# The first output unit of a hybrid attention layer computed in fp32 from unscaled inputs, and one more row tile turned by DMA

## The reference, cut to what matters

```python
h = x * rsqrt(mean(x*x) + 1e-6) * norm_pre_g          # x: 512 rows x 1024, fp32
u = h @ w_in                                          # 1024 x 4096, eight groups of 512 columns
dq, dk, dv, dg, mq, mk, mv, mg = split(u)
a = rmsnorm(softmax-difference attention(dq, dk, dv) + bias) * silu(dg)
b = block attention(mq, mk, mv) + bias, * silu(mg)
out = x + rmsnorm(concat(a, b) @ w_out) * norm_post_g
```

## Time and profile before

| | |
|---|---|
| median of 3 executions | 257.85 us (257.16 to 259.13) |
| the profiled execution | 258.5 us, span of its trace 256.7 us |
| TensorE (PE) busy | 246.4 us, 96% |
| VectorE (DVE) busy | 174.9 us, 68% |
| ScalarE (ACT) busy | 144.4 us, 56% |
| GpSimd (POOL) busy | 32.9 us, 13% |

### The profile page before, as it was taken

One profiled execution on the slowest core, in us unless ns is written; L12 is line 12 of the kernel. 1 busy time (PEld: TensorE's weight loads), 2 busy tenths in 40 slices (PEclk: granted clock), 3 DMA queues, 4 the chain that ended last, 5 costly groups with the idle time before them and its releaser, 6 DMA issues.

```text
span 256.7 us, 4437 instructions
## 1 busy us (share of the span) xinstructions
PE 246.4 (96%) x1589; PEld 123.5 (48%) x1589; DVE 174.9 (68%) x382; ACT 144.4 (56%) x337; POOL 32.9 (13%) x77
## 2 busy tenths in 40 slices
PE   6899999999999999999989999999999999999990
PEld 6544444445444545544455444444444444554570
DVE  1787766367559688868787777867888784936313
ACT  3986557156365667574676686485677553721110
POOL 2139300000000230041041041000000000110101
PEclk9999999999999999999999999999999999999997
DMA  6979997897045434534535763586569954596222
GB/s 221 402 250 243 277 277 282 250 360 213 21 51 138 146 112 132 122 106 112 107 110 132 121 189 103 125 221 149 146 162 184 248 148 79 99 164 206 47 84 83
DMA packets 59626, 42.47 MB, mean 165 GB/s; under 512 B 45760, under 2 KB 46024, under 8 KB 59604
## 3 DMA queue, kind: packets, MB, share of 16 engines
q1 hardware_dynamic: 59604, 42.19, 62.0%
HBM read 29.04 MB, written 2.13 MB: 121 GB/s over the span
## 4 chain that ended last, share of the span: by engine, by line
PE 70%; DVE 8%; ACT 8%; DMA 8%; issue 3%; SPq 1%; POOL 1%; DVEq 0%; POOLq 0%; ACTq 0%
PE unit_ps L562 57%; PE score_ps L597 5%; PE o_ps L618 4%; DMA pt<-arena 4%; DMA stage<-in_w_in_dram 3%; ACT arena L747 2%; PE unit_ps L578 2%; ACT w_hi L707 2%; DVE w_lo L840 2%; ACT junk L693 1%; DVE w_lo L838 1%; ACT w_hi L706 1%; DVE arena L917 1%; SPq L378 1%; PE score_ps L670 1%
## 5 line engine op out<-in xcount | busy, mean ns | idle before, releaser
L562 PE MATMUL unit_ps<-area,w_hi 128*128 128x512 f16 x256 | 76.2, 380 | 0.0
L562 PE MATMUL unit_ps<-w_hi,area 128*128 128x512 f16 x224 | 70.5, 380 | 0.9 <-DVE w_lo L840 0.8
L747 ACT ACTIVATE arena<-arena,negmax 128x512 f32<-128x512 f32 (+3 forms) x64 | 35.4, 554 | 44.2 <-DVE negmax L917 44.0
L562 PE MATMUL unit_ps<-area,w_lo 128*128 128x512 f16 x128 | 48.5, 379 | 0.0
L562 PE MATMUL unit_ps<-w_lo,area 128*128 128x512 f16 x112 | 42.5, 379 | 0.0
L562 PEld LDWEIGHTS unit_ps<-area,w_hi 128*128 128x128 f16 x256 | 24.0, 98 | 27.3 <-issue 1.1
L562 PEld LDWEIGHTS unit_ps<-w_hi,area 128*128 128x128 f16 x224 | 21.8, 98 | 27.3 <-issue 2.0
L917 DVE CUSTOM_DVE_ANT_0 arena<-score_ps,strips 128x512 f32<-128x512 f32 (+3 forms) x64 | 28.6, 485 | 8.5 <-PE score_ps L597 8.3
L838 DVE SCALAR_TENSOR_TENSOR w_lo<-stage,g_cols,w_hi 128x512 f16<-128x512 f32 x32 | 24.2, 756 | 14.0 <-ACT w_hi L707 13.8
L706 ACT ACTIVATE w_hi<-stage,g_cols 128x512 f16<-128x512 f32 x32 | 22.7, 711 | 7.7 <-DMA stage<-in_w_in_dram 7.6
L840 DVE SCALAR_TENSOR_TENSOR w_lo<-stage,g_cols,w_hi 128x512 f16<-128x512 f32 x32 | 24.9, 777 | 0.0
(11 more groups left out here) (98 smaller groups left out, 334.2 us busy)
## 6 DMA issues: line engine op xcount, KB each, us to landing
stage<-in_w_in_dram SPq DMA_DIRECT2D x32, 512.0 KB, 4.2
stage<-in_w_out_dram SPq DMA_DIRECT2D x8, 512.0 KB, 3.8
arena<-in_x_dram SPq DMA_DIRECT2D x4, 512.0 KB, 7.7
strips<-bias_rows SPq DMA_DIRECT2D x1, 2048.0 KB, 11.8
stage<-in_x_dram SPq DMA_DIRECT2D x4, 512.0 KB, 3.5
out_dram<-area SPq DMA_DIRECT2D x3, 512.0 KB, 3.3
strips<-bias_rows SPq DMA_DIRECT2D x1, 1024.0 KB, 8.8
g_row<-in_norm_post_g_dram SPq DMA_DIRECT2D x1, 512.0 KB, 12.4
```

What stands on the lines that cost most here:

```text
L562: last = nc.tensor.matmul(bank, a, b, start=(k == 0 and n == 0), stop=(k == KT - 1 and n == 2))
L747: nc.scalar.activation(probs[:, i % 2, m, 0:n], probs[:, i % 2, m, 0:n], ACT.Exp, bias=negmax[:, i, m:m + 1], scale=-1.0, accum_out=sums[: ...
```

## The change

- Unit 0 is 8 fp32 products (`first_quarter`): x tile 0 is transposed by TensorE as loaded (no row factor), VectorE multiplies it by `g_cols` on the way out of PSUM into `x_first` (`x_weigh`), and the moving operand is the weights as loaded, in the stage buffers. The row factor (times 1/64, `first_scale`) is applied when the unit is evicted. Loads 4 to 7 also wait until the unit has read the stage.
- `ht` of tile 0 is no longer made on this way: tile 0 is scaled, split and turned by DMA like tiles 2 and 3, after them; it is first read by unit 4.
- Unit 1 takes its high products first, quarter by quarter, like units 2 and 3 (`late_lower_unit`).
- All four row tiles have their squares shared between ScalarE and VectorE.
- The warm-up products are 5 and 2 in place of 8, 2 and 8; tile 0's transposes wait for x alone.
- norm_pre_g is loaded from ScalarE's queue. The loads of lambda and of the subln weights stand behind the transposes of tile 0, and VectorE's dot products of lambda follow unit 3. Splits in the prologue come a unit later.

Its core:

```diff
-    WARM_UP = (8, 2, 8)
+    WARM_UP = (5, 2)
...
-    SPLIT_AT_UNIT = [[4], [5, 6], [7], [8, 9], [10], [11, 12], [13]]
+    SPLIT_AT_UNIT = [[], [4], [5, 6], [7], [8, 9], [10, 11], [12, 13]]
...
-    X_PARTS = [2] + [1] * (TILES - 1)
...
+    X_TURNED = [2, 3, 0]
...
+        x_first = gates[:, 1, 0:2, :].rearrange("p t (k s) -> p (t k) s", s=P)
+        def x_columns(t):
+            return score_ps[:, 2 * t:2 * t + 2, :].rearrange("p b (k s) -> p (b k) s", s=P)
+        def x_half_rows(t):
+            return x_halves[:, t % 2, :, :]
...
             def load_quarter(n):
                 if n >= 4:
                     sp.wait_ge(split_lo, n - 3)
+                if 4 <= n < 7:
+                    sp.wait_ge(first_read, n - 3)
+                elif n == 7:
+                    sp.wait_ge(unit_done, 1)
...
             def turn_x(t, h):
...
+                sp.wait_ge(xn_lo_ready if h else xn_hi_ready, X_TURNED.index(t) + 1)
+                sp.dma_start_transpose(ht[:, h, :, t * P:(t + 1) * P], x_half_rows(t)[:, h, :])\
+                    .then_inc(x_turned[t][h], 16)
...
@@ -392,16 +398,18 @@
...
             with nc.allow_non_contiguous_dma(reason="32 x 12 table, transposed once"):
                 sp.dma_start(rel_t, rel_bias.rearrange("b h -> h b")).then_inc(rel_loaded, 16)
-            sp.dma_start(lam_in[:, :, :], diff_lambda[0].partition_broadcast(P)).then_inc(small_loaded, 16)
-            sp.dma_start(subln[:, :], diff_subln_g[0].partition_broadcast(P)).then_inc(small_loaded, 16)
...
             for h in range(2):
                 turn_x(2, h)
             load_quarter(6)
+            for h in range(2):
+                turn_x(3, h)
             load_quarter(7)
             for h in range(2):
-                turn_x(3, h)
+                turn_x(0, h)
+            sp.dma_start(lam_in[:, :, :], diff_lambda[0].partition_broadcast(P)).then_inc(small_loaded, 16)
+            sp.dma_start(subln[:, :], diff_subln_g[0].partition_broadcast(P)).then_inc(small_loaded, 16)
             load_quarter(8)
             sp.wait_ge(row_built, 1)
             sp.dma_start(bias_rows.ap(), row_sb).then_inc(rows_stored, 16)
...
...
-                                            ALU.add, ALU.mult).then_inc(x_mean, 1)
+                pool.wait_ge(x_half_squared, t + 1)
+                nc.gpsimd.tensor_tensor(x_ms[:, t:t + 1], x_sq[:, t:t + 1], x_half_sq[:, t:t + 1], ALU.add)\
+                    .then_inc(x_mean, 1)
                 pool.wait_ge(x_mean, t + 1)
                 nc.gpsimd.tensor_tensor(x_rstd[:, t:t + 1], x_ms[:, t:t + 1], minus_half[:, 0:1],
                                         ALU.pow).then_inc(x_rstd_ready, 1)
+                if t == 0:
+                    pool.wait_ge(x_rstd_ready, 1)
+                    nc.gpsimd.tensor_scalar(first_scale[:, :], x_rstd[:, 0:1], U_SCALE, 1.0, ALU.mult,
+                                            ALU.mult).then_inc(first_scale_ready, 1)
...
+            def x_transposes(t, ks, done):
+                for k in ks:
+                    last = nc.tensor.transpose(score_ps[:, 2 * t + k // 4, (k % 4) * P:(k % 4 + 1) * P],
                                                x_sb[:, t, k * P:(k + 1) * P], ident[:, :])
-                last.then_inc(xt_ready, 1)
+                last.then_inc(done, 1)
...
+                        for t in (range(TILES) if kind in "qk" else [i]):
+                            if t == 1:
+                                pe.wait_ge(ht_ready, 1)
+                            else:
+                                pe.wait_ge(x_turned[t][0], 16)
+                                pe.wait_ge(x_turned[t][1], 16)
...
-                if (u, q) == (0, 2):
-                    pe.wait_ge(ht_ready, 2)
                 pe.wait_ge(split_lo, 4 * g + q + 1)
...
-            def turned_unit(u):
+            def first_quarter(q):
+                pe.wait_ge(x_first_ready, q // 2 + 1)
+                pe.wait_ge(w_loaded[q], 16)
+                for k in (2 * q, 2 * q + 1):
+                    cols = slice(k % 2 * WIDTH, (k % 2 + 1) * WIDTH)
+                    last = nc.tensor.matmul(unit_ps[:, 0, :], x_first[:, k, :], stage[:, q, cols], start=(k == 0),
+                                            stop=(k == KT - 1))
+                last.then_inc(first_read if q < 3 else unit_done, 1)
+            def late_lower_unit(u):
                 _, half, i, g = unit_of(u)
                 bank = unit_ps[:, u % 2, :]
                 rows = slice(i * P, (i + 1) * P)
-                pe.wait_ge(unit_freed, u - 1)
-                pe.wait_ge(split_lo, 4 * (g + 1))
-                for h, b in ((0, w_hi), (0, w_lo), (1, w_hi)):
-                    if b is w_hi:
-                        pe.wait_ge(x_turned[i - 2][h], 16)
-                    for k in range(KT):
-                        last = nc.tensor.matmul(bank, ht[:, h, k, rows], b[:, g % 3, k, :],
-                                                start=(k == 0 and h == 0 and b is w_hi), stop=(k == KT - 1 and h == 1))
+                if u >= 2:
+                    pe.wait_ge(unit_freed, u - 1)
+                if i == 1:
+                    pe.wait_ge(ht_hi_ready, 1)
+                else:
+                    pe.wait_ge(x_turned[i][0], 16)
+                for q in range(4):
+                    pe.wait_ge(split_lo, 4 * g + q + 1)
+                    for k in (2 * q, 2 * q + 1):
+                        for b in (w_hi, w_lo):
+                            nc.tensor.matmul(bank, ht[:, 0, k, rows], b[:, g % 3, k, :],
+                                             start=(k == 0 and b is w_hi), stop=False)
+                if i == 1:
+                    pe.wait_ge(ht_ready, 1)
+                else:
+                    pe.wait_ge(x_turned[i][1], 16)
+                for k in range(KT):
+                    last = nc.tensor.matmul(bank, ht[:, 1, k, rows], w_hi[:, g % 3, k, :], start=False,
+                                            stop=(k == KT - 1))
                 last.then_inc(unit_done, 1)
...
             warm_up(WARM_UP[1])
-            for part in range(X_PARTS[0]):
-                x_transposes(0, part)
-            warm_up(WARM_UP[2])
+            pe.wait_ge(x_loaded[0], 16)
+            for part in range(2):
+                x_transposes(0, range(part * KT // 2, (part + 1) * KT // 2), x_first_turned)
             for q in range(4):
-                unit_quarter(0, q)
-                if q == 1:
-                    x_transposes(1)
-            for q in range(4):
-                unit_quarter(1, q)
-            turned_unit(2)
-            turned_unit(3)
+                first_quarter(q)
+                if q == 2:
+                    pe.wait_ge(xs_ready, 1)
+                    x_transposes(1, range(KT), xt_ready)
+            for u in range(1, TILES):
+                late_lower_unit(u)
...
+                elif u == 0:
+                    act.wait_ge(first_scale_ready, 1)
+                    ins = nc.scalar.activation(v_hi[:, 0, 0:WIDTH], src, ACT.Copy, scale=first_scale[:, :])
...
+            def x_hi():
+                act.wait_ge(xt_ready, 1)
+                nc.scalar.activation(ht[:, 0, :, P:2 * P], x_columns(1), ACT.Copy).then_inc(ht_hi_ready, 1)
...
             def xn_hi(t):
                 act.wait_ge(x_rstd_ready, t + 1)
-                nc.scalar.activation(x_halves[:, t - 2, 0, :], x_sb[:, t, :], ACT.Copy,
+                if t == 0:
+                    for h in range(2):
+                        act.wait_ge(x_turned[2][h], 16)
+                nc.scalar.activation(x_half_rows(t)[:, 0, :], x_sb[:, t, :], ACT.Copy,
                                      scale=x_rstd[:, t:t + 1]).then_inc(xn_hi_ready, 1)
...
-                square(x_sq[:, t:t + 1], x_sb[:, t, 0:DM // X_PARTS[t]], x_squared, t + 1)
+                square(x_sq[:, t:t + 1], x_sb[:, t, 0:DM // 2], x_squared, t + 1)
+            nc.scalar.dma_start(g_rows[:, :], norm_pre_g[0].rearrange("(k p) -> k p", p=P)).then_inc(gpre_loaded, 16)
             x_square(0)
             split(0)
-            x_hi(0, 0)
-            x_hi(0, 1)
             split(1)
             x_square(1)
             split(2)
             split(3)
             x_square(2)
-            x_hi(1)
+            x_hi()
             xn_hi(2)
             x_square(3)
             for u in range(FIRST_UNITS):
-                if u == 1:
-                    xn_hi(3)
                 for n in SPLIT_AT_UNIT[u]:
                     split(n)
                 unit(u)
-                if u == 2:
+                if u == 0:
+                    xn_hi(3)
+                if u == 1:
+                    xn_hi(0)
+                if u == 4:
                     act.wait_ge(lam_dots, 2)
                     nc.scalar.activation(lam_exp[:, :], lam_dot[:, :], ACT.Exp).then_inc(lam_exps, 1)
...
+                    scale = first_scale[:, :] if u == 0 else Q_SCALE if kind == "q" else U_SCALE
+                    ins = nc.vector.scalar_tensor_tensor(lo, src, scale, hi, ALU.mult, ALU.subtract)
```

(91 more changed lines are left out.)

41 lines of the change are left out of this document (6 added, 35 removed).

## The result

The changed kernel took 262.16 us (260.5 to 266.17, 6 runs) against 258.24 for the kernel before: 1.0136 of it, 95% interval 1.0096 to 1.0177. It is slower by some 3.5 to 5 us, where no measurable change was forecast. Both profiles show the same waits, in the first of 1.4 and 3.2 us where e1 has 1.85 and 2.59.

What follows compares the result with a forecast made beforehand. TensorE was taken as the bound, so unit 4's start decides: 1.2 us sooner, less 0.1 for late weights, sums to -1.1 us, 256.8 against the median of 257.85; range 255.3 to 259.0.

Steps and rivals of the forecast that it cites:

- the last term of the forecast: Load 11 behind the strips: issued at 32.5, landing 42.3, split by 44.9, wanted by unit 6 at 45.9; charged 0.1 us.
- the 1 us that I added: Bias rows on GpSimd, started after the last row factor, were expected about 1 us later than in the kernel before.
- The rule itself: Unit 6's last quarter: load 11 begins to cost once it lands after 43.3, slower than before once after 44.5.
- Rival 3: Unit 6's last quarter waits for load 11 behind the strips, landing at 46.3: +1.8 us, 259.7; chance 0.13.
- signs of being wrong: Unit 4 starting before 30.8 or after 32.5, or a wait of over 1 us between 40 and 50 us.
- The fp32 unit: Unit 0 on TensorE: about 0.87 us a product, 7.0 us for the unit against 5.18, done at 14.7.
- rival 4: Clock stays at 1.2 GHz under the fp32 unit: +4.7 us, 262.6; only the first quarter slow, +1.7; chance 0.05.
- First gate: Unit 2 waits for turned tile 2, starting at 20.3 to 21.0, 1.2 to 1.9 us before its 22.19.
- Second and third gate: Unit 3 waits about nothing, up to 1.8 us, for tile 3; tile 0 for unit 4 lands 29.9 to 32.5.
- rival 2: Queue blocks at tile 0's transposes, landing 32.5 to 33.5, taking the gain: -0.3 to +0.7 us, 258.0; chance 0.18.
- Forecast of the start of unit 4: Unit 4, the first reading all four row tiles, starts at about 31.6, 1.2 us before 32.84.

Runs made afterwards that it cites:

- e1: The changed kernel measured and profiled again, nothing edited: 1.0195 of the kernel before.
- e6: The kernel before, with only the loads of lambda and subln moved behind tile 3's transposes and lambda's dot products after unit 3: 1.0032 of before.
- e7: The changed kernel with tile 0 transposed by TensorE between units 2 and 3 instead of by DMA, fp32 unit kept: 0.998 of the kernel before.
- e2: The changed kernel with the second strips issued head by head in slots 2 to 9 and norm_post_g in slot 11: 1.0014 of the kernel before.
- e9: The changed kernel with the loads of lambda and subln back in their old place, ahead of load 4: 0.9998 of the kernel before.
- e5: The kernel before, without fp32 unit, with a spare transpose pair behind tile 3's, lambda and subln loads behind it, dot products after unit 3: 1.0172 of before.
- e4: The changed kernel with load 11 issued ahead of the first strips instead of behind them: 0.9986 of the kernel before.
- e8: The changed kernel with VectorE's half squares of tiles 2 and 3 moved ahead of split 2 and of x_lo: 1.016 of the kernel before.
- e3: The kernel before, with the second strips issued head by head in slots 2 to 9 and norm_post_g in slot 11: 0.9986 of before.
- e10: The kernel before, with load 11 ahead of the first strips and the second strips spread over slots 2 to 9: 1.0005 of before.
- e11: The changed kernel with load 11 ahead of the first strips, second strips spread, half squares of tiles 2 and 3 early: 0.9926 of the kernel before.
- e12: The kernel of e7 with load 11 ahead of the first strips, second strips spread, half squares of tiles 2 and 3 early: 0.9918 of before, 256.53 us.

## Why the prediction was wrong, point by point

**The step that failed** is the last term of the forecast, the load behind the strips, "hidden with 1.0 us to spare" and charged at 0.1. I put load 11's issue at 32.5 and its landing at 42.3; it was issued at 37.06 and landed at 46.4. Three terms were too small.

- Tile 0's transposes began issuing at 26.16, about 1 us later than I had it, and the pair held the queue 4.39 us, not 2.7, as the pair of the earlier trace rows that took 4.92 had warned (+1.7). This is not a wait for VectorE, which had written the low half by 26.9.
- The bias rows' way through memory was not in my sum at all as something that grows: 4.5 us from issue to strips against 2.2 before (+2.2). With the small loads in their new place it took 3.7 to 5.2 in ten profiles, with them in the old one 1.9 to 3.3 in four. In e6 only they were moved, and it went from 2.2 to 5.0. I had counted the time to issue them, 1 us, and nothing behind it.
- GpSimd builds the bias rows later than the 1 us that I added: until 21.30 + 9.61 = 30.9 instead of 27.9, for it starts 2.0 us later and takes 1.0 longer. Here this cost nothing, since the queue reached the store at 32.18 only. In e7, where the queue is free, the store goes at 29.96, just after the rows are built.

```profile
21.30 9.61 POOL L477 COPY gates<-gates 12x1 f32<-12x1 f32 x32
```

The first two make 4.9 us, for the 4.6 by which load 11 was late. The rule itself was right. I had said that it costs from a landing at 43.3 on with unit 4 at 31.6, so 11.7 us behind the start of unit 4. That gives 44.7 in e1, and a landing at 46.4 should cost 1.7: TensorE waits 1.85. In e2 it gives 43.6 and the load lands at 35.98 + 8.2 = 44.2: 0.6, and 0.7 is seen. In e6 (44.4 for 45.6) and e9 (43.1 for 44.6) nothing waits.

**Rival 3 was the case** that came, with a chance of 0.13 and +1.8. Its landing at 46.3 is the measured one by luck: I had both pairs hold the queue 2.0 us longer, but tile 3's held it 2.67, as in my sum, and the rest came from the start and the bias rows. Its price was too low because I followed the delay only to unit 6. Behind load 11 stand loads 12 to 17 and then 2 MB of strips, and these meet the first transpose of probabilities (2.6 us, e2), which in turn costs 1.7 us of clock. I had not asked what the delayed queue carries into next. That the queue makes the loss without the fp32 unit is shown by e5 and e7, that it takes both the pair and the small loads by e6 and e9, and that its two waits are one chain by e4. Both of my signs of being wrong came: unit 4 after 32.5, and a wait of over 1 us between 40 and 50.

**The fp32 unit: right.** Records come 0.43 us apart, (1.88 - 0.59) / 3, so 0.86 a product against 0.87. It ran from 7.09 to 15.4 instead of 6.3 to 14.7; the transposes ahead of it took 1.91 us, not 1.09, still at the low clock (rival 4 in its small form). That cost nothing, as unit 2 waited anyway.

**First gate: right in kind, 0.7 to 1.4 us late.** I had unit 2 wait for the turned tile 2, from 20.3 to 21.0; it started at 21.71. The trace puts the wait down to unit 0's low half on VectorE, but that had been written 0.8 us earlier:

```profile
18.34 1.28 DVE L950 SCALAR_TENSOR_TENSOR pt<-arena,x_rstd,pt 128x1024 f16<-128x1024 f32 x1 [0.49 <-ACT pt L806]
19.55 0.69 DVE L924 CUSTOM_DVE_ANT_0 heads_out<-arena 128x512 f32<-128x512 f32 x1
...
20.16 0.75 DVE L915 SCALAR_TENSOR_TENSOR v_lo<-unit_ps,first_scale,v_hi 128x512 f16<-128x512 f32 x1
```

The low half is there at 20.9. The first transpose of tile 2, issued at 18.34, lands 3.3 us later, at 21.64, and unit 2 starts at 21.71:

```profile
area<-pt SPq DMA_TRANSPOSE x1, 3.3
```

In e9 the low half is there at 20.9 too and unit 2 starts at 21.72, and there the trace does not name VectorE. In e2, e4 and e7 unit 2 starts 0.1 us behind the landing of the same transpose as well (21.56, 21.65, 21.52). So my expectation of e8, that VectorE's list is this gate, was wrong; its early squares brought tile 2's transpose forward, to 17.05. The gate came late because tile 2's factor did: it was ready at 17.1, where I had 15.7 to 16.5.

**Second and third gate: right.** Tile 3 cost nothing. Tile 0 held unit 4 for 0.8 us (the trace puts this wait down to issue; in e8 it names the transfer), until 32.98; I had 31.6, and rival 2, a queue that blocks at tile 0's transposes, gave a landing at 32.5 to 33.5. That rival came true as well; in e2, where the pair held the queue for less, unit 4 did not wait and started at 31.92.

**Forecast of the start of unit 4.** By place it was missed by 1.4 us. As a difference it came near: against 33.7 to 34.1 in three profiles of kernels that are the one before up to there (e3, e10) or nearly (e6), the changed kernel of e1 gains 0.7 to 1.1. One profile gave me a base 0.8 to 1.3 us early. The place moves from profile to profile in the changed kernel too (31.92 in e2, 32.98 in e1, 33.48 in the first), and it is not the whole time: e3 has the span of the kernel before, 256.7, with a start 0.8 later. With the queue mended, e11 and e12 are 2.0 and 2.4 us below the median of the kernel before. The earlier unit 4 accounts for 0.8 to 1.6 of that; the rest I have not traced.

## What to carry to other kernels

When a change adds instructions to an in-order DMA queue, follow every transfer behind them to the end of the prologue, with its deadline, not only to the first place where it may be late: here one transfer put back by 6.5 us started a chain of loads, strips and transposes that cost 5 us, and moving a single 512 KB load past a 1 MB one gave all of it back. Two edits to a queue can each be harmless and lose time together, once they use up the slack (e6, e9, e5). A slack of 1 us in a sum of ten estimated terms is no slack. Where a trace names an engine that had finished earlier, look for a transfer that landed just before the start. Take starting points from more than one profile.

## What the runs showed of the hardware

- A wait of 2.6 us (e1) on a TensorE that had been busy for 16.5 us let the granted clock fall to 0.50 for 3.4 us, beginning some 0.9 us after work had begun again. So did the 2.2 us in e8 (0.50 from 70 to 72). After 2.1 us in e9, 1.7 in e6, 1.2 in e5 and 0.9 in e4 it stayed at 1.00. What decides between them these runs do not show.
- The store of 30 KB of bias rows to memory took, until the next DMA could use it, 2.2 us in the kernel before, 1.9 and 2.0 in e3 and e10, 3.3 in e9, and 3.7 to 5.2 in the ten profiles where the loads of lambda and subln stand just ahead of load 8.
- A pair of 128 x 1024 fp16 DMA transposes held the issuing queue 2.6 us at the least (e7) and 5.4 at the most (e6, of it 0.3 waiting for VectorE). What stands ahead does not settle it: in e1 two pairs, each behind a 512 KB load and another pair, held it 2.67 and 4.39, and tile 0's pair held it 3.10 in e2, 3.70 in e4 and 4.59 in e9. The pairs of tile 3 and tile 0 together held it 7.1 us in e1, and in e5 those of tile 3 and the spare one 7.4, where tile 3's alone held it 4.9 in the kernel before.
